# Four to eighteen products of the identity with itself at five places of a one-core decoder block in float32

## The reference

```python
x = x + parallel_head_groups(rms_norm(x, g_mix[l]), positions, ...)      # one projection, 4 + 6 + 6 heads, w_out
x = x + memory_cross_attention(rms_norm(x, g_xmem[l]), rms_norm(mem, g_mem[l]), ...)  # 4 heads, 256 memory tokens, w_mo
x = x + routed_expert_ffn(rms_norm(x, g_ffn[l]), w_router[l], b_router[l], ...)       # 32 experts, the best 4 of each token
```

```python
hh = jnp.einsum("td,edf->tef", xc, w_e1) + b_e1
glu = jnp.minimum(hh[..., 0::2], SWIGLU_LIMIT)
lin = jnp.clip(hh[..., 1::2], -SWIGLU_LIMIT, SWIGLU_LIMIT)
act = glu * jax.nn.sigmoid(SWIGLU_ALPHA * glu) * (lin + 1.0)
act = act * gc[..., None].astype(act.dtype)
return jnp.einsum("tef,efd->td", act, w_e2) + gc.astype(b_e2.dtype) @ b_e2
```

## Time and profile before

| | us |
|---|---|
| median of 3 runs | 1171.39 |
| the runs | 1168.49, 1171.39, 1177.49 |
| time of the profiled execution | 1169.88 |
| its span, first to last instruction | 1168.3 |
| TensorE busy in it | 1103.7 (94%) |
| DVE, ACT, GpSimd (POOL) busy | 315.6, 192.3, 128.4 |
| mean granted clock of TensorE | 0.988 |
| read from memory | 428.72 MB |

### The profile page before, as it was taken

The page is one execution under the profiler, slowest core; times in us unless marked ns, Lnnn a source line. Parts: engine busy times, 40 slices in busy tenths (PEclk is TensorE's granted clock), DMA queues, the critical chain, the costliest instruction groups (busy, mean ns, idle before and its releaser), DMA issues.

```text
span 1168.3 us, 13535 instructions
## 1 busy us (share of the span) xinstructions
PE 1103.7 (94%) x5024; PEld 444.2 (38%) x5024; DVE 315.6 (27%) x665; ACT 192.3 (16%) x388; POOL 128.4 (11%) x287
## 2 busy tenths in 40 slices
PE   6989979889999999999999999999999999999997
PEld 4656855643333333333333333333333333333332
DVE  4463643441111222112212211111111111111112
ACT  2133332411111111111111111111111111111111
POOL 1020200011111111111111111111111111111100
PEclk9989989989999999999999999999999999999999
DMA  6913345559999999999999999999999999999995
GB/s 243 346 36 134 120 140 215 240 199 404 429 427 427 427 428 429 429 428 429 427 430 427 429 427 429 429 429 427 429 429 429 427 429 430 429 427 429 430 428 228
DMA packets 45975, 430.09 MB, mean 368 GB/s; under 512 B 8352, under 2 KB 15776, under 8 KB 21120
## 3 DMA queue, kind: packets, MB, share of 16 engines
q1 hardware_dynamic: 43024, 427.67, 87.5%
q10 hardware_dynamic: 2928, 2.11, 0.6%
HBM read 428.72 MB, written 1.05 MB: 368 GB/s over the span
## 4 chain that ended last, share of the span: by engine, by line
PE 62%; DMA 31%; DVE 4%; ACT 1%; issue 1%; DVEq 0%; SPq 0%; ACTq 0%
DMA ring<-in_w_e_dram 30%; PE banks L655 25%; PE banks L675 12%; PE banks L283 11%; PE banks L599 4%; PE banks L626 4%; PE banks L688 2%; PE banks L607 1%; PE banks L271 1%; DMA w_in_cq<-in_w_in_dram 1%; PE banks L317 1%; PE banks L300 1%; PE banks L615 0%; PE banks L299 0%; PE banks L638 0%
## 5 line engine op out<-in xcount | busy, mean ns | idle before, releaser
L655 PE MATMUL banks<-ring,xg_T 128*64 128x512 f32 x2048 | 478.7, 599 | 17.5 <-DMA ring<-in_w_e_dram 15.6
L655 PEld LDWEIGHTS banks<-ring,xg_T 128*64 128x64 f32 x2048 | 134.8, 136 | 300.7 <-issue 254.9
L675 PE MATMUL banks<-ring,act_T 128*64 128x512 f32 x1024 | 235.6, 597 | 6.1 <-DMA ring<-in_w_e_dram 6.1
L1691 DVE TENSOR_TENSOR x_sb<-x_sb,banks 128x1024 f32<-128x1024 f32 x64 | 78.2, 1221 | 380.1 <-PE banks L626 372.7
L675 PEld LDWEIGHTS banks<-ring,act_T 128*64 128x64 f32 x1024 | 69.2, 137 | 143.4 <-issue 119.2
L1701 DVE TENSOR_TENSOR glu<-banks,b_T 128x512 f32<-128x512 f32 x32 | 22.1, 692 | 329.4 <-PE banks L688 329.4
L626 PE MATMUL banks<-y_sb,hot_gate_T 64*128 64x512 f32 x256 | 72.0, 640 | 1.7 <-ACT hot_gate_T L1237 1.7
L971 POOL COPY picked<-slot_table 128x2 f32 (+1 forms) x32 | 6.3, 198 | 562.3 <-PE banks L615 562.3
L1220 ACT COPY hidden<-banks 128x1024 f32<-128x1024 f32 x32 | 32.4, 1012 | 206.6 <-PE banks L655 206.6
L1206 ACT COPY xg_rows<-banks 128x512 f32<-128x512 f32 x33 | 19.3, 586 | 277.7 <-PE banks L599 277.7
L599 PE MATMUL banks<-h_sb,hot_slot 128*64 128x512 f32 x264 | 63.7, 604 | 1.3 <-DVE hot_slot L1662 1.3
(11 more groups left out here) (279 smaller groups left out, 789.6 us busy)
## 6 DMA issues: line engine op xcount, KB each, us to landing
ring<-in_w_e_dram SPq DMA_DIRECT2D x190, 2048.0 KB, 39.0
w_out_sb<-in_w_out_dram SPq DMA_DIRECT2D x1, 4096.0 KB, 13.3
ring<-in_w_e_dram SPq DMA_DIRECT2D x4, 1024.0 KB, 41.1
w_in_qk<-in_w_in_dram SPq DMA_DIRECT2D x1, 2048.0 KB, 14.5
w_mkv_sb<-in_w_mkv_dram SPq DMA_DIRECT2D x1, 2048.0 KB, 11.3
w_in_cq<-in_w_in_dram SPq DMA_DIRECT2D x1, 1536.0 KB, 12.1
w_in_qc<-in_w_in_dram SPq DMA_DIRECT2D x1, 1536.0 KB, 17.4
w_in_kc<-in_w_in_dram SPq DMA_DIRECT2D x1, 1536.0 KB, 15.6
```

The costliest lines, as they stand in the source:

```text
L655: ins = TE.matmul(PS[SLOTS * h:SLOTS * h + SLOTS, B_W1 + b, :], left, ring[slot][:, 2 * F * j + F * h + 512 * b:2 * F * j + F * h + 512 * ...
L675: ins = TE.matmul(PS[SLOTS * h:SLOTS * h + SLOTS, B_W2, :], actT[:, c % 4, c // 4, :], ring[slot][:, D * j + 512 * h:D * j + 512 * h + 512 ...
L1691: V.tensor_tensor(X[:, t, :], X[:, t, :], PS[:, first:first + 2, :].rearrange("p b n -> p (b n)"), ALU.add).then_inc(S("added"), 1)
```

## The change

A helper of TensorE multiplies the identity (128 x 128, in SBUF) by itself n times. The results go to the next bank of the ring of transposes and are never read. Ahead of them the helper waits until that bank is free. It takes no bank from the ring, so that the next transposes go to the same one and overwrite it. It is called at five places, with 4, 12, 18, 7 and 4 products. Nothing else differs; code behind it moves down by some lines.

```diff
+        def keep_busy(n):
+
+            if turn.n >= 4:
+                pe.wait_ge(S("turned_out"), turn.n - 3)
+            for _ in range(n):
+                TE.matmul(PS[:, turn.n % 4, 0:P], ident[:], ident[:], start=True, stop=True)
+
...
         project("qc", 0)
+        keep_busy(4)
         pe.wait_ge(S("logf_wide"), 1)
...
         for h in range(FOX_H):
+            if h == 2:
+                keep_busy(12)
             bank = into(f"bias{h}")
...
         turn_p("d0")
+        keep_busy(18)
         pe.wait_ge(S("groups_normed"), 1)
...
         mem_values(0)
+        keep_busy(7)
         mem_out(0)
...
         pe.wait_ge(S("rows_gained"), NT)
+        keep_busy(4)
         gather(0)
```

## The result

The changed kernel takes 1167.43 us (median of 18 runs, 1164.89 to 1169.64), the kernel before 1174.71 us (median of 18 runs, 1168.49 to 1180.57). The ratio is 0.9941, with a 95% interval of 0.9924 to 0.9958: 6.9 us faster, between 4.9 and 8.9. The scatter changed with it: the runs of before spread over 12.1 us, those of the changed kernel over 4.8 us.

What follows compares the result with a forecast made beforehand. DMA's weight stream sets the later pace, its start tied to TensorE's front, partly at half clock. Terms -3.35 - 1.3 - 1.65 + 0.4 = -5.9 us gave 1164.0 or 1165.5 by starting time, taken as 1164.8; range 1160.5 to 1170.0.

Steps and rivals of the forecast that it cites:

- The way to the end: From the first product with expert weights (251.62 us) on: front gains move the weight stream's start and the end equally.
- the rival of the hidden front: The weight stream would start or end where it did, hiding the shorter front: 1170.6 us; chance 0.04.
- The prices of the added work: First four places: 0.9, 2.7, 4.1 and 1.6 us of products fit in their waits at full clock, costing nothing.
- The slower rival: Overrun: at half clock the 12 and 18 products outlast their waits, the last 4 are late; 1175.6 us, chance 0.04.
- the central case: The forecast itself, a measured time of 1162.8 to 1167 us; chance 0.55.
- place 3: 18 products before the transposes of the normed groups; gain of 1.3 us, limited by ACT's copies.
- the next stretch: Half-clock stretch at 188 to 191 us, no products put before it; counted 0, with 1.65 us either way.
- Places 1 and 2: 4 products before `cum`, 12 before `bias2`; clock stays at 1.00, gain of 3.35 us.
- place 4: 7 products before `mem_out(0)`, which then runs at full clock; gain of 1.65 us.
- Place 5: 4 products ahead of the first gather, clock already at half; loss of 0.4 us, bounds -0.9 and +0.8.
- The ceiling: All five half-clock stretches of the front together cost at most 10.8 us, 0.9% of the time.
- the clock falls all the same: Rival: identity products do not hold the clock at places 2, 3, 4; 1166.5 to 1171 us; chance 0.20 (some or all).

Runs made afterwards that it cites:

- the narrow products: Changed kernel with each added product 4 columns wide instead of 128, same numbers at all five places; ratio to the kernel before 1.0009 (0.9985 to 1.0032).
- the eleven places: Changed kernel with six more places, 15 products instead of 12 before `bias2`, 25 instead of 18 before the groups; median 1161.26 us, ratio to before 0.9883.

## Why the prediction was right, and where not

**The way to the end** held. In all 14 traces the eleventh load is issued between 251.47 and 264.67 us, and from there to the end of the span it is 910.8 to 911.6 us in every one. What the front gains arrives, to within 0.8 us; the rival of the hidden front falls.

**The clock as the cause** held: the gain goes with the time at half clock, from kernel to kernel and within one kernel, and the narrow products, which do not raise the clock, bring nothing. **The prices of the added work** held: in the trace the four waits kept 0.58, 0.89, 1.68 and 0.50 us, where the text had 0.6, 0.9, 1.6 and 0.7, and nothing overran. The slower rival did not show.

**The sum** of 5.9 us lies in the measured 4.9 to 8.9, in its lower half, but not by its terms, so that its agreement is partly luck. The forecast time, 1164.8, was set from a first median of before, 1171.39, that came out 3.3 us higher in 18 runs; the measured 1167.43 is 2.6 us over it and just outside the 1162.8 to 1167 of the central case, inside the range. The mis-sized term is place 3: forecast 1.3 us, measured 5.8 (3.3 to 8.1) by itself. Its mechanism was right for the trace it was worked out from (1.15 us there). The error was to take one execution's stretch, 6.8 us with 3.58 of work in it, for the kernel's. In other traces the stretch is up to 13.7 us long and reaches into the first product with `w_out`, which no ACT copy limits, and the next stretch, which the text counted as 0, can go with it. Places 1 and 2 (2.2 us, forecast 3.35) and place 4 (1.4, forecast 1.65) agree within their intervals. Place 5 brings nothing that can be measured, where +0.4 was forecast. The single gains add up to 11 us with wide intervals, the change brought 6.9; whether they overlap stays open.

**The ceiling** was wrong. "That is the ceiling for any such change", 10.8 us, was half of TensorE's work in the stretches of one mild execution. On the mean the kernel before spends 47.1 us at half clock, not 27, and the eleven places took 13.8 us away. That is 1.2% of the time, so the prediction's "The rows agree" on a cost under 1% held for that one execution only.

**The rival "the clock falls all the same"** happened, in the profile: 1.68 us of idle time were left behind the 18 products, and the clock fell at 159.1. There it lay over 6.7 us of work. Together with the 10 us around the gather this is why the trace of the changed kernel has the first product with expert weights at 250.98 and not at the 245.7 of the text. From place to place between the two traces: places 1 and 2 gained 3.3 us up to the end of `qc1` (forecast 3.35), place 3 lost 1.6 up to the end of the first product with `w_out` (forecast: a gain of 1.3), place 4 gained 1.7 (forecast 1.65), and from there to the first product with expert weights 1.8 were lost. Besides, this execution was 0.9 us late before anything was changed (the last transposes before `qc0` start at 68.12 instead of 67.17): the first product of the latents took 13.32 us in it and 12.02 in the trace of before. That forecast of the profile was wrong, though the median moved by more than was said.

**Two signs** that the text named and did not price: the runs of before spread over 9 us, and its profiled execution was 1.5 us under their median. Both said that the trace could be on the mild side, and that each term was "a mean over cases".

**A slip** in the rival of the overrun: 12 products outlast a wait of 3.58 us as soon as a third of them run at half clock (2.7 us and a third of 2.7 make 3.6), and 18 outlast theirs at two fifths, not two thirds. The rival did not happen, so nothing hung on it.

## What to carry to other kernels

Where the times of one program go with its mean granted clock, as here, one trace gives one draw of the cost; before pricing, look at the mean clock of many executions, and at how far the times scatter. Filling a wait has to be tried in its amount: 9 products in a wait of 5.7 us brought nothing, 18 brought 5.8 us, and small ones in the same number, at all five places, brought nothing. Fill with work that is certain to end before the wait does, and look for the short waits too: six more, of 0.6 to 2.6 us, with a few products added at two old places, were worth another 5.6 us.

## What the runs showed of the hardware that was not expected

- In two traces of each of two kernels the stretches of half clock are at the same places (within 0.7 us), while the timed executions of the kernel before range from 28 to 61 us at half clock.
- At the start TensorE runs at half clock although the column shows 1.00. In the trace of before the first products of the latents begin like this:

```profile
13.95 3.31 PE L283 MATMUL banks<-w_in_cq,h_T 128*128 128x384 f32 x5 [2.64 <-DMA w_in_cq<-in_w_in_dram]
```
